# Projected queries of token blocks 1 and 2 alternate between two pairs of PSUM banks, one step ahead of the key scores

## What is computed

```
def peer_block(xb, w_q, subkeys, u_tab, v_tab):
    q = jnp.einsum('nd,de->ne', xb, w_q).reshape(n, PEER_HEADS, 2, PEER_SUBKEY_DIM)   # 8 heads, 2 x 128
    s = jnp.einsum('nhcd,hckd->nhck', q.astype(jnp.float32), subkeys.astype(jnp.float32))  # 128 keys each
    s1, i1 = lax.top_k(s[:, :, 0], PEER_TOPK)
    s2, i2 = lax.top_k(s[:, :, 1], PEER_TOPK)
    ...
    eidx = jnp.take_along_axis(cidx, pos, axis=-1)       # 16 of 16384 experts for each token and head
    g = jax.nn.softmax(top, axis=-1)
    u = u_tab[eidx]
    act = jax.nn.gelu(jnp.einsum('nd,nhkd->nhk', xb, u).astype(jnp.float32), approximate=False) * g
    return jnp.einsum('nhk,nhkd->nd', act.astype(xb.dtype), v_tab[eidx])
```

## Time and profile before

| | |
|---|---|
| three runs | 2553.94, 2554.8 and 2559.31 us, median 2554.8 us |
| profiled execution, its own time | 2557.82 us |
| its span in the trace | 2556.1 us |
| TensorE / VectorE / GpSimd / ScalarE busy | 91% / 57% / 25% / 15% of the span |
| DMA | 861.41 MB, mean 337 GB/s |
| TensorE's granted clock, mean | 0.969 |

### The profile page before, as it was taken

One profiled execution on the slowest core, in us unless ns is written; L12 is line 12 of the kernel. 1 busy time (PEld: TensorE's weight loads), 2 busy tenths in 40 slices (PEclk: granted clock), 3 DMA queues, 4 the chain that ended last, 5 costly groups with the idle time before them and its releaser, 6 DMA issues.

```text
span 2556.1 us, 29215 instructions
## 1 busy us (share of the span) xinstructions
PE 2325.6 (91%) x11802; PEld 1688.2 (66%) x11802; DVE 1468.8 (57%) x2342; ACT 379.9 (15%) x657; POOL 642.0 (25%) x470
## 2 busy tenths in 40 slices
PE   8999999988988948888799798999999999999991
PEld 8999999956734848787789798644444444444440
DVE  3333333343676777677699396254555555555558
ACT  3333333331102101000023131000000000000001
POOL 2000000000132343222203112233333434434332
PEclk9999999998998979999999899999999999999996
DMA  6443344365996999999999999999999999999995
GB/s 255 144 141 139 140 140 142 144 251 211 383 402 262 408 368 404 421 414 421 421 377 364 424 394 391 386 417 411 413 418 410 409 411 412 414 410 409 396 393 208
DMA packets 129924, 861.41 MB, mean 337 GB/s; under 512 B 14752, under 2 KB 14880, under 8 KB 33824
## 3 DMA queue, kind: packets, MB, share of 16 engines
q1 hardware_dynamic: 63360, 425.88, 42.0%
q0 software_dynamic: 56960, 408.97, 39.5%
q10 hardware_dynamic: 9504, 25.17, 2.5%
HBM read 833.75 MB, written 26.21 MB: 336 GB/s over the span
## 4 chain that ended last, share of the span: by engine, by line
DMA 43%; PE 34%; DVE 12%; issue 5%; POOL 4%; ACT 1%; DVEq 0%; SPq 0%; ACTq 0%; POOLq 0%
DMA scratch<-peer_v,idx_v 25%; DMA arena<-peer_u,idx_u 14%; PE bank L1255 7%; DVE scratch L1660 5%; PE bank L1097 4%; PE bank L975 4%; PE bank L976 3%; PE bank L979 3%; PE bank L1238 3%; POOL arena L580 2%; PE bank L997 2%; PE bank L993 2%; PE bank L994 2%; DMA cache<-u_tiles 2%; DMA arena<-peer_v,idx_v 1%
## 5 line engine op out<-in xcount | busy, mean ns | idle before, releaser
L1599 DVE CUSTOM_DVE_ANT_0 arena<-arena,x 128x2048 f32<-128x2048 f32 x256 | 584.7, 2292 | 211.7 <-DMA arena<-peer_u,idx_u 211.6
L580 POOL DMA_INDIRECT arena<-peer_u,idx_u x256 | 346.4, 1353 | 714.6 <-DVE dots L1599 673.2
L1660 DVE SCALAR_TENSOR_TENSOR scratch<-scratch,gate 128x2048 f32<-128x2048 f32 x112 | 263.3, 2351 | 379.2 <-DMA scratch<-peer_v,idx_v 378.8
L595 POOL DMA_INDIRECT scratch<-peer_v,idx_v x112 | 228.9, 2044 | 465.6 <-DVE scratch L1660 446.9
L1255 PE MATMUL bank<-scratch,cache 128*128 128x128 f32 x2048 | 250.4, 283 | 57.2 <-DMA cache<-u_tiles 57.2
L1255 PEld LDWEIGHTS bank<-scratch,cache 128*128 128x128 f32 x2048 | 241.9, 198 | 63.8 <-DMA cache<-u_tiles 63.7
L1255 PE MATMUL bank<-scratch,ln_rows 128*128 128x128 f32 x2048 | 241.0, 277 | 34.0 <-DMA ln_rows<-u_tiles 32.2
L1311 DVE TENSOR_TENSOR arena_rounded<-arena,w_high 128x1024 fp32r<-128x1024 f32 x96 | 114.5, 1230 | 266.4 <-ACT w_high L662 266.4
L1255 PEld LDWEIGHTS bank<-scratch,ln_rows 128*128 128x128 f32 x2048 | 233.1, 192 | 39.8 <-DMA ln_rows<-u_tiles 37.7
L1278 PE MATMUL bank<-ln_rows,scratch 128*128 128x512 f32 x512 | 230.1, 592 | 0.7 <-ACT scratch L840 0.7
L1278 PE MATMUL bank<-cache,scratch 128*128 128x512 f32 x512 | 230.0, 592 | 0.0
(11 more groups left out here) (210 smaller groups left out, 2875.5 us busy)
## 6 DMA issues: line engine op xcount, KB each, us to landing
ln_rows<-u_tiles SPq DMA_DIRECT2D x64, 1024.0 KB, 14.2
cache<-u_tiles SPq DMA_DIRECT2D x64, 1024.0 KB, 14.2
ln_rows<-peer_v SPq DMA_DIRECT2D x64, 1024.0 KB, 9.6
cache<-peer_v SPq DMA_DIRECT2D x64, 1024.0 KB, 9.1
arena<-w_heads SPq DMA_DIRECT2D x32, 1024.0 KB, 5.0
arena<-w_out SPq DMA_DIRECT2D x24, 1024.0 KB, 8.2
arena<-w_heads SPq DMA_DIRECT2D x8, 2048.0 KB, 8.6
arena<-w_q SPq DMA_DIRECT2D x16, 1024.0 KB, 8.7
```

The costliest lines, as they stand in the source:

```text
L580: pool.indirect_dma_start(out=u_row[k % U_SLOTS], out_offset=None, in_=peer_u, in_offset=bass.IndirectOffsetOnAxis(ap=idx_u[:, p % 2, k:k ...
L595: pool.indirect_dma_start(out=v_row[slot], out_offset=None, in_=peer_v, in_offset=bass.IndirectOffsetOnAxis(ap=idx_v[:, q % 2, k:k + 1], a ...
L1599: dve.tensor_tensor_reduce(u_row[slot], u_row[slot], x1[:, 0 if p < H else 2, :], 1.0, 0.0, ALU.mult, ALU.add, dots[:, p % 2, k:k + 1]).th ...
L1660: dve.scalar_tensor_tensor(out=residual2, in0=v_row[slot], scalar=coef[:, GROUPS_DENSE + q, k:k + 1], in1=residual2, op0=ALU.mult, op1=ALU ...
```

## The change

The queries of group 1 get two pairs of PSUM banks: even steps use banks 4 and 5 as before, odd steps banks 0 and 1 (free by then: they held output sums that VectorE has read). On TensorE the scores of step `j - 1` are issued after the projections of step `j`, and those of step 3 at the very end. A projection from step 2 on waits only until its own pair has been emptied, two steps back. Since `queryT` has room for one step only, ScalarE's `copy_query` of steps 1 to 3 now first waits for the scores of the step before (`key_scored[1][i] >= j`). Group 0 keeps its banks and its order. No other queue's instructions change; the number of matmuls, copies and DMAs stays the same.

```diff
--- before.py
+++ after.py
@@ -330,6 +330,11 @@
         ln2_step, ln2_weighted, ln2_sd, ln2_scaled, y_ready, y_stored = (
             sem("ln2_step"), sem("ln2_weighted"), sem("ln2_sd"), sem("ln2_scaled"), sem("y_ready"), sem("y_stored"))
 
+        def query_bank(grp, j, i):
+            if grp == 0:
+                return 4 + i
+            return 4 - 4 * (j % 2) + i
+
         block = ctx.enter_context(nc.Block())
 
 
@@ -787,7 +792,9 @@
 
                 n = len(GROUPS[grp]) * P
                 act.wait_ge(query_done[grp], j * 4 + 2 * i + 2)
-                act.activation(queryT[:, i, 0:2 * n], bank[4 + i][:, 0:2 * n], ACT.Copy)\
+                if grp == 1 and j:
+                    act.wait_ge(key_scored[grp][i], j)
+                act.activation(queryT[:, i, 0:2 * n], bank[query_bank(grp, j, i)][:, 0:2 * n], ACT.Copy)\
                    .then_inc(query_copied[grp][i], 1)
 
             def copy_keys(grp, j, i):
@@ -1118,10 +1125,13 @@
             def project_query(grp, j, i, c, slot):
 
                 n = len(GROUPS[grp]) * P
-                if c == 0:
+                if c == 0 and grp == 0:
                     pe.wait_ge(query_copied[grp][i], j + LEAD)
+                elif c == 0 and j >= 2:
+                    pe.wait_ge(query_copied[grp][i], j - 1 + LEAD)
+                out = bank[query_bank(grp, j, i)]
                 for t in range(DT):
-                    mm = pe.matmul(bank[4 + i][:, c * n:(c + 1) * n], slot[:, t * P:(t + 1) * P], x1T[grp][:, t, :],
+                    mm = pe.matmul(out[:, c * n:(c + 1) * n], slot[:, t * P:(t + 1) * P], x1T[grp][:, t, :],
                                    start=(t == 0), stop=(t == DT - 1))
                 mm.then_inc(query_done[grp], 1)
 
@@ -1209,8 +1219,11 @@
                         m = j * 4 + 2 * i + c
                         pe.wait_ge(ring_loaded[m % RING], ((16 + m) // RING) * 16 + 16)
                         project_query(1, j, i, c, wq_slot[m % RING])
-                for i in range(2):
-                    score_keys(1, j, i)
+                if j:
+                    for i in range(2):
+                        score_keys(1, j - 1, i)
+            for i in range(2):
+                score_keys(1, 3, i)
 
             def turn_picks(b):
```

## The result

| | before | changed |
|---|---|---|
| median, runs taken side by side | 2554.37 us (2551.82 to 2559.31, 4 runs) | 2578.55 us (2574.1 to 2587.6, 4 runs) |
| profiled execution, its own time / span | 2557.82 / 2556.1 us | 2578.91 / 2577.2 us |
| first expert tile (L1255, now L1268) | 977.53 us | 956.45 us |
| turn 4, first dot to last | 947.2 to 998.7, 51.5 us | 952.2 to 1022.7, 70.6 us |
| TensorE's wait ahead of tile 70 ends | 1307.75 | 1330.05 |

The ratio of the runs is 1.0094, 95% interval 1.0071 to 1.0118: the changed kernel is slower by about 24 us, where 16 was forecast. The spans differ by 21.1 us.

A forecast was written before the change was run, and what follows sets the result against it. The prediction took the DMA engines, at 422 GB/s, to bound this stage. Its terms, +1 + 14.5 - 1.2 + 1.5 = +15.8 us on a median of 2554.8, gave about 2571 us, range 2556 to 2582.

The forecast's parts named there:

- main case: The forecast itself: tile 70 comes 15.8 us later, median about 2571 us, bounds 2563 to 2578; chance 0.70.
- rival B: At weigh(2), all 12.6 us of VectorE's wait stay and the lead adds 14.5: 2582 us; chance 0.09.
- TensorE's gap: Before the first expert tile: step 3's projection fills the 34 us idle time; the tile starts 26 us earlier, about 951.5.
- The stall at `weigh(2)`: In turn 3, VectorE waits 12.6 us for activate(2) but mostly catches up: +1 us, bounds 0 and 12.6.
- The lead meets the gathers: In turn 4, dots beside earlier tile loads take 4.97 us each: +14.5 us, bounds 10 and 17.
- The bound by bytes: Upper bound in turn 4: nine tiles of lead, 22.4 us of DMA time less 5.3 us free, +17.
- What comes back: At the end of turn 7, tile loads stop and last dots run faster: -1.2 us, bounds 0 and -5.
- A cold TensorE: At tile 70, TensorE runs slower after standing over 25 us: +1.5 us, bounds 0 and 2.
- After tile 70, carried unchanged: From tile 70 to the end, the shift at tile 70 was carried through unchanged; last stage some 16 us later.
- A: In turn 7, the last dots run fast and return about 14.5 us: 2556 us; chance 0.12.
- C: At tile 70, TensorE arrives 26 us earlier and goes on, so the lead reaches the end: 2529 us; chance 0.06.
- D: At step 3's projection, another wait keeps TensorE's gap open: 2555 us, or the stall alone; chance 0.03.

The follow-up runs named there:

- e1: The changed kernel with activate(2) ahead of copy_keys(1) on ScalarE; 2573.66 us, 1.0078 of the kernel before.
- e5: The kernel before with the placing of picks at expert tiles 78 and 102 instead of 70 and 94; 2557.82 us, 1.0008 of the kernel before.
- e4: The changed kernel with the placing of picks at expert tiles 78 and 102 instead of 70 and 94; 2552.23 us, 0.9990 of the kernel before.
- e9: The changed kernel with expert tile 2 held until four dots of turn 4 are done; 2573.64 us, 1.0077 of the kernel before.
- e2: The changed kernel with expert tile 2 held until ten dots of turn 4 are done; 2560.74 us, 1.0020 of the kernel before.
- e3: The changed kernel with activate(2) ahead of copy_keys(1) and tile 2 held for ten dots of turn 4; 2558.74 us, 1.0015 of the kernel before.
- e7: The kernel before, one pair of banks, with activate(3) after queries(2) and queries(3) on ScalarE; 2571.82 us, 1.0075 of the kernel before.
- e6: The changed kernel with activate(2) ahead of copy_keys(1) and placing at tiles 78 and 102; 2545.19 us, 0.9966 of the kernel before.
- e8: The kernel before with activate(3) after queries(3) on ScalarE and placing at tiles 78 and 102; 2546.32 us, 0.9967 of the kernel before.

## Why the prediction was right, and where it was off

The direction, the main mechanism and the range (2556 to 2582) held; the size was 24.2 us where 15.8 was forecast. The upper bounds of the terms add up to +20, so the loss lies above even these. The 2563 to 2578 given for the main case were counted from the profiled execution's 2557.8; counted like the forecast, from the median of 2554.8, they are 2560 to 2575, and 2578.55 is outside. What kept the range right was the rival B at its upper end. Two terms were too small, the stall and above all the lead. Terms against the traces, where a difference of 3 us is within what two traces of the same instructions show:

- **TensorE's gap (start at 951.5): 956.45.** The 5 us are the later end of turn 3, and so are most of the 12.19 us of gap left where about 6 were worked out. The tail from `activate(3)` to the first tile took 956.45 - 946.26 = 10.2 us, as summed.
- **The stall at `weigh(2)` (+1): about +4.** It happened where it was said, 10.9 us at 898 for 12.6. Turn 3 started 1.7 us later in this execution and its last dot 5.0 later, ending at 946.2 where 940 to 943 was said, and e1 took 3.5 off. The mis-sized step is the pace afterwards. The ninth dot came at 920.95 as worked out, but the seven intervals behind it took 22.96 us where 2.65 each would be 18.6: two of them were over 4.5 us (before 925.97 and before 938.00). I had the undisturbed pace throughout. That GpSimd sends one by one for four slots that emptied at once (its rows at 912.12, 916.48, 928.53 and 940.57 are 2.75 to 3.05 us long, others 0.94 to 2.15) would explain it; no run here tests that.
- **The lead meets the gathers (+14.5, upper bound 17): +19.1.** The eleven intervals took 54.65 us instead of 40.2, +14.4, as forecast. Landing on it so closely is partly luck: in e5 they took 43.5 us without any lead, in e4 55.0. The missing 4.6 us lie ahead of them. I let the fifth dot keep its place, and in the text above even allowed for less while the loads "ramp up". In fact four tiles are asked for in a burst, since TensorE already held tiles 0 and 1, and the fifth dot's rows stood behind them. e9 shows that. The bound by bytes, +17, was nearer, and still low: the lead was ten tiles, not nine (tile 15 starts at 1025.48, just behind the last dot of turn 4, where tile 5 did before). Ten tiles by the same sum give 24.9 - 5.3 = +19.6.
- **What comes back (-1.2): -1.8, but not there.** From turn 4's last dot (24.1 us late) to turn 7's (22.3) the delay fell by 1.8 us. The hold ahead of tile 68 came as described, 15.48 us, but the last dots of turn 7 gained nothing: they still came every 4.97 us, one interval excepted, with the DMA engines full (share 1.01 from 1270 to 1293), and the last eleven intervals took 55.65 us against 55.20 before. The delay shrank in turns 5 and 6. The term's number is luck, its reason failed.
- **A cold TensorE (+1.5): +1.4.** The first interval of dots behind tile 70 took 7.25 us (1329.97 to 1337.22) against 5.8 before; its tile took 5.30 us against 3.74 for the same tile before. The granted clock had been 0.55 from 1304 to 1330, while TensorE stood; before the change it was 1.00 ahead of tile 70.
- **After tile 70, carried unchanged: not quite.** Between tile 70 and the last stage 2.9 us more were lost, of which the interval above is 1.4. The last stage started 25.2 us late and the span ended 21.1 late. That stage took 930.8 us before and 926.7 after, and between 924.4 and 931.2 in e1, e2, e3 and e7, with no relation to the edits that I can see. The median moved by 24.2, so no gain from this is claimed.
- **The rivals.** A (the last dots give it back) fell: the waits for ScalarE's banks capped the lead at tile 68, with loads up to tile 71, and the last dots kept their slow pace. B (the full stall stays) fell by e1, though turn 3 did end late, which the prediction gave as B's sign. C fell by the 25.99 us at tile 70. Even with the wait moved eight tiles on, the gain was not C's 26 us against the kernel before, but none that can be measured in e4, and 9 us in e6. D fell by the rows at 907.03.
- **Rules of the Trainium skill.** The ceiling that the Trainium skill gives (DMA: Bandwidth & Descriptors, Where 436 GB/s comes from), 435 GB/s, would have made the eleven intervals 53.0 us, an estimate from that page; they took 54.65, so the measured 422 GB/s was the better figure. The Trainium skill (Perfetto Trace Analysis, Identifying the Most-Contended Engine) says to optimize the most-contended engine first, but for TensorE it rules out the matmul busy share as the measure. Here that share is the 91%, while weight loads are busy for 66%, and in this stage the DMA engines moved 421 GB/s at a share of 1.01. Going by the 91% led the wrong way: filling TensorE's gap slowed this kernel three times (the change, e1, e7), until the wait at tile 70 was moved.

## What to carry to other kernels

A gap on the busiest engine is worth closing only if something later needs that engine's lead; look for the next place where it meets another engine, and who arrives there last. An earlier start of an engine is also an earlier start of its loads, and where the DMA engines are full, these are paid for by whoever gathers beside them: here 2.5 us for each tile of 1.05 MB. If a lead has been won, the fixed positions further on have to be set again. Here neither the lead nor the new positions alone beat the kernel before, and the two kernels that did (e6, e8) had both and no stall at `weigh(2)`.

When a copy is moved behind a later product, everything queued behind it on its engine moves as well. Here that was one small gelu: VectorE stood 11 us for it, and 3.5 to 5 of them were never made up.

## What the runs showed of the hardware

Gathers sent for by GpSimd and tile loads sent for by SyncE shared the DMA engines about evenly in the changed kernel: from 976 to 1028 one queue moved 10.90 MB and the other 10.93, one tile of each every 4.97 us, 421 GB/s together. A burst of loads delays a gather as well. The gather for the fifth dot was sent for at 954.72, just ahead of four tile loads (from 955.61 on), and its dot came 13.4 us later. In e9, where the loads were held until 961.79, the same gather went out at 954.58 and its dot came after 8.7 us without a wait.
